# Probability blocks moved inside SBUF in 16 transfers on two queues, with two turn buffers and a lag of two

## The reference, cut to what matters

```python
s = jnp.einsum('bqgjd,bkgd->bgjqk', q5, kw)
p = masked_softmax(s, mw[None, None, None])
o_win = jnp.einsum('bgjqk,bkgd->bqgjd', p.astype(vw.dtype), vw)
...
o = g[..., 0:1] * o_cmp + g[..., 1:2] * o_sel + g[..., 2:3] * o_win
```

## Time and profile before

| | |
|---|---|
| median of 3 runs | 618.28 us |
| the profiled execution | 616.48 us, of which the span is 614.7 us |
| PE busy in the span | 565.3 us, 92% |
| DVE, ACT, POOL busy | 55%, 43%, 14% |
| p_turn written to DRAM | 16 units x 4 transfers, 64 KB to 256 KB each |
| read back | 16 transfers, 256 KB to 1 MB each |

### The profile page before, as it was taken

How to read it: one execution, slowest core, us unless ns; L and a number is a source line. 1 busy time by engine, 2 the same in 40 slices (tenths; PEclk the granted TensorE clock), 3 DMA queues, 4 the chain that set the end, 5 groups by cost and what they waited for, 6 DMA issues and landing times.

```text
span 614.7 us, 12596 instructions
## 1 busy us (share of the span) xinstructions
PE 565.3 (92%) x5102; PEld 506.0 (82%) x5102; DVE 335.5 (55%) x826; ACT 266.1 (43%) x601; POOL 88.6 (14%) x145
## 2 busy tenths in 40 slices
PE   6899999999889999988999998998895999998993
PEld 4899999999788998886897785766573999997992
DVE  5632213787776672364374575665663347762265
ACT  5543435446223433442332676466573342222333
POOL 0015432121101223603300000000001000000000
PEclk9999999999879999999999998999897999999998
DMA  8347822452334244842822177777685533307103
GB/s 296 153 120 231 263 69 95 165 187 87 104 100 178 81 129 144 278 159 89 290 69 70 40 202 239 220 219 225 200 227 127 143 90 86 111 12 238 38 2 145
DMA packets 70026, 90.98 MB, mean 148 GB/s; under 512 B 5457, under 2 KB 57873, under 8 KB 69714
## 3 DMA queue, kind: packets, MB, share of 16 engines
q1 hardware_dynamic: 59520, 55.34, 29.6%
q0 software_dynamic: 9728, 33.72, 16.5%
q10 hardware_dynamic: 722, 1.12, 0.5%
HBM read 75.71 MB, written 18.61 MB: 153 GB/s over the span
## 4 chain that ended last, share of the span: by engine, by line
PE 41%; DMA 11%; DVE 9%; ACT 3%; SPq 3%; issue 2%; ACTq 0%; DVEq 0%
PE m L1649 29%; DMA p_dram<-p_turn 9%; DVE p_turn L1560 3%; SPq L768 3%; PE t L1858 1%; PE s L1831 1%; PE s L1832 1%; PE s L1834 1%; DMA U<-in_x_p 1%; PE t L1795 1%; PE o L1917 1%; DVE w_lo L1231 1%; DMA p_slot<-p_dram 1%; PE s L1872 1%; PE o L1963 1%
## 5 line engine op out<-in xcount | busy, mean ns | idle before, releaser
L1649 PE MATMUL m<-h_hi,w_hi 128*128 128x272 f32 x448 | 135.1, 302 | 0.5 <-DVE w_lo L1231 0.5
L1649 PE MATMUL m<-h_hi,w_lo 128*128 128x272 f32 x448 | 130.1, 290 | 0.0
L1649 PE MATMUL m<-h_lo,w_hi 128*128 128x272 f32 x448 | 129.7, 290 | 0.0
L1649 PE MATMUL m<-w_hi,h_hi 128*128 128x256 f32 (+2 forms) x360 | 104.6, 291 | 4.4 <-DVE U L1597 2.0
L1649 PE MATMUL m<-w_lo,h_hi 128*128 128x256 f32 (+2 forms) x360 | 101.9, 283 | 0.0
L1649 PE MATMUL m<-w_hi,h_lo 128*128 128x256 f32 (+2 forms) x360 | 101.9, 283 | 0.0
L1231 DVE TENSOR_TENSOR w_lo<-raw,w_hi 128x1024 fp32r<-128x1024 f32 (+2 forms) x62 | 71.2, 1154 | 46.4 <-ACT w_hi L962 46.3
L1649 PEld LDWEIGHTS m<-h_hi,w_hi 128*128 128x128 f32 x448 | 85.4, 191 | 12.9 <-issue 10.4
L1649 PEld LDWEIGHTS m<-h_lo,w_hi 128*128 128x128 f32 x448 | 85.6, 191 | 0.0
L1649 PEld LDWEIGHTS m<-h_hi,w_lo 128*128 128x128 f32 x448 | 85.4, 191 | 0.0
L1649 PEld LDWEIGHTS m<-w_hi,h_hi 128*128 128x128 f32 (+1 forms) x360 | 67.9, 189 | 6.2 <-DVE U L1597 2.3
(11 more groups left out here) (304 smaller groups left out, 950.2 us busy)
## 6 DMA issues: line engine op xcount, KB each, us to landing
raw<-in_w_in SPq DMA_DIRECT2D x36, 512.0 KB, 4.5
U<-in_x_p SPq DMA_DIRECT2D x8, 512.0 KB, 7.3
p_dram<-p_turn SPq DMA_DIRECT2D x16, 256.0 KB, 5.1
raw<-in_w_o SPq DMA_DIRECT2D x8, 512.0 KB, 3.7
U<-p_dram POOLq DMA_DIRECT2D x3, 1024.0 KB, 6.3
p_dram<-p_turn SPq DMA_DIRECT2D x16, 192.0 KB, 4.8
U<-p_dram POOLq DMA_DIRECT2D x3, 768.0 KB, 5.1
raw<-in_w_in SPq DMA_DIRECT2D x8, 256.0 KB, 3.4
```

The source lines that it names most:

```text
L1649: ins = mm(out, lhs(a, k), rhs(b, k), start=(k == 0 and a + b == 0), stop=(k == n - 1 and a == 1))
```

## The change

The trip through DRAM goes. Square rows of the turn buffer (32 partitions: quarter a) go straight to quarter b of the slot. For each of the 16 pairs (a, b) there is one transfer of 32 partitions x (number of blocks) x 128 elements; SP issues ten of them (b = 0, 1 and half of 2), POOL six, each on semaphores of its own, and whoever waits for a unit waits for both. There are two turn buffers; the second takes the place of the fourth slot, so there are three slots. `pp` (u) is put two rounds after `ps` (u) instead of three.

```diff
-LAG = 3
+LAG = 2
+NSLOT, BY_SYNC = 3, 10
...
-LAST_TURN = (0, 1, 2)
+LAST_TURN = (1, 2)
...
+        def block_move(u, n):
+            b, a = divmod(n, 4)
+            kt = UNITS[u][0] + 1
+            src = p_turn[u % 2][32 * a:32 * a + 32, 0:512 * kt].rearrange("p (k b n) -> p k b n", k=kt, b=4)[:, :, b, :]
+            dst = slot[u % NSLOT][32 * b:32 * b + 32, 0:512 * kt].rearrange("p (k a n) -> p k a n", k=kt, a=4)[:, :, a, :]
+            return dst, src
+        def wait_moved(eng, u):
+            eng.wait_ge(p_moved[u % NSLOT], 16 * BY_SYNC * (u // NSLOT + 1))
+            eng.wait_ge(p_moved_pool[u % NSLOT], 16 * (16 - BY_SYNC) * (u // NSLOT + 1))
...
-                    sp.wait_ge(p_turned, u + 1)
-                    for a in range(4):
-                        sp.dma_start(p_dram[u, 0:nb, :, a * P:(a + 1) * P].rearrange("b j r -> j b r"),
-                                     p_turn[32 * a:32 * a + 32, 0:nb * P].rearrange("j (b r) -> j b r", b=nb)).then_inc(p_written, 16)
+                    sp.wait_ge(p_turned, s[1] + 1)
+                    for n in range(BY_SYNC):
+                        sp.dma_start(*block_move(s[1], n)).then_inc(p_moved[s[1] % NSLOT], 16)
...
-                    pool.wait_ge(p_written, 64 * (u + 1))
-                    pool.dma_start(slot[u % 4][:, 0:512 * (i + 1)].rearrange("p (k n) -> p k n", k=i + 1),
-                                   p_dram[u, 0:4 * (i + 1), :, :].rearrange("(k b) j n -> (b j) k n", b=4)).then_inc(p_moved[u % 4], 16)
+                    pool.wait_ge(p_turned, s[1] + 1)
+                    for n in range(BY_SYNC, 16):
+                        pool.dma_start(*block_move(s[1], n)).then_inc(p_moved_pool[s[1] % NSLOT], 16)
...
-                            dve.wait_ge(p_used, u - 3)
+                            dve.wait_ge(p_used, u - NSLOT + 1)
...
-                    dve.wait_ge(p_written, 64 * u)
+                    if u >= 2:
+                        wait_moved(dve, u - 2)
...
-                        pe.wait_ge(p_moved[u % 4], 16 * (u // 4 + 1))
+                        wait_moved(pe, u)
```

More of the change, by code:

```diff
@@ L553, in nsa_gmlp_layer @@
         SEL, WIN, CMP = 0, 1056, 1600
-        slot = [U[:, 0:2048], U[:, 2048:4096], U[:, 4096:6144],
-                nc.alloc_sbuf_tensor_at("p_slot", [P, 2048], F32, offset=wsT_at)[:, :]]
+        slot = [U[:, 0:2048], U[:, 2048:4096], U[:, 4096:6144]]
         pb = [x.rearrange("p (j k) -> p j k", j=J) for x in slot]
         p_blocks = [x.rearrange("p (k a j g r) -> p k a j g r", k=NT, a=4, j=2, g=G) for x in slot]
-        p_turn = nc.alloc_sbuf_tensor_at("p_turn", [P, 2048], F32, offset=prm_at)
+        p_turn = [nc.alloc_sbuf_tensor_at("p_turn0", [P, 2048], F32, offset=prm_at),
+                  nc.alloc_sbuf_tensor_at("p_turn1", [P, 2048], F32, offset=wsT_at)]
         ctb = [pm("b_sp"), tmp[:, :, :].rearrange("p a c -> p (a c)")[:, 0:512]]
-        p_dram = nc.dram_tensor("p_dram", [len(UNITS), 4 * NT, 32, 512], F32).ap()
         cp = U[:, 6144:6144 + J * G * NCP]
@@ L593, in nsa_gmlp_layer @@
         pads_zero, st_ready, mix_fn, pv_part = sem("pads_zero"), sem("st_ready"), sem("mix_fn"), sem("pv_part")
-        p_weight, p_turned, p_written, p_used, c_used = sem("p_weight"), sem("p_turned"), sem("p_written"), sem("p_used"), sem("c_used")
-        p_moved = [sem(f"p_moved{n}") for n in range(4)]
+        p_weight, p_turned, p_used, c_used = sem("p_weight"), sem("p_turned"), sem("p_used"), sem("c_used")
+        p_moved = [sem(f"p_moved{n}") for n in range(NSLOT)]
+        p_moved_pool = [sem(f"p_moved_pool{n}") for n in range(NSLOT)]
         ssq_ready, root_in, root_done, h_ready = sem("ssq_ready"), sem("root_in"), sem("root_done"), sem("h_ready")
@@ L1130, in _ @@
                     for j in range(J):
-                        ins = nc.scalar.activation(pb[u % 4][:, j, 0:n], pb[u % 4][:, j, 0:n], ACT.Exp, bias=st[:, m + 4 + j:m + 5 + j],
+                        ins = nc.scalar.activation(pb[u % NSLOT][:, j, 0:n], pb[u % NSLOT][:, j, 0:n], ACT.Exp, bias=st[:, m + 4 + j:m + 5 + j],
                                                    scale=SCALE, accum_out=st[:, m + 8 + j:m + 9 + j])
@@ L1556, in _ @@
                     dve.wait_ge(p_scaled, u + 1)
-                    dve.wait_ge(p_written, 64 * u)
+                    if u >= 2:
+                        wait_moved(dve, u - 2)
                     for j in range(J):
-                        dst = p_turn[:, 0:nb * P].rearrange("p (b j r) -> p b j r", b=nb, j=J)[:, :, j, :]
-                        ins = v.transpose(dst, pb[u % 4][:, j, 0:32 * nb].rearrange("p (b r) -> p b r", b=nb))
+                        dst = p_turn[u % 2][:, 0:nb * P].rearrange("p (b j r) -> p b j r", b=nb, j=J)[:, :, j, :]
+                        ins = v.transpose(dst, pb[u % NSLOT][:, j, 0:32 * nb].rearrange("p (b r) -> p b r", b=nb))
                     ins.then_inc(p_turned, 1)
```

12 lines of the change are left out of this document (4 added, 8 removed).

## The result

The changed kernel takes **636.32 us**, median of 4 runs (633.89 to 639.19), where the kernel before took 619.34 in the same comparison: a ratio of 1.0267 with a 95% interval from 1.0205 to 1.0330. It is slower, and its median lies above the forecast range of 611 to 633. Its profiled execution took 637.37 us, with a span of 635.6.

What follows compares the result with a forecast made beforehand. PE was the largest part, its DMA stage paced by the ring of turn, four issues, last landing, next turn. Stretches summed to -0.9 us, the clock added 4.4: 616.5 + 3.5 = 620.0 profiled, 621.8 us median, range 611 to 633.

Steps and rivals of the forecast that it cites:

- The move takes 0.03 + 9 spacings + landing: From a turn's end until `pp` may start, SP's ten transfers decide: 7.3, 7.0, 6.7 and 6.4 us for four to one block.
- Landing of 3.0 to 2.1 us: Time from an SP transfer's issue start to its landing: 3.0, 2.7, 2.4 and 2.1 us for four to one block.
- rival B: Moves are quick, spacing near 0.34 and landing 2 us or less: 607 to 612, say 611 us; chance 0.18.
- POOL's six end earlier: POOL's six transfers of a move take 5.5 us and end before SP's ten, even with another 0.5 us.
- The ring of two rounds: From `pp` (u) to `pp` (u + 2): 14.8 us with two blocks, 12.9 with one, slower than the ring it replaces.
- -3.7 us to the turn of unit 4: Four-block stretch: the turn of unit 4 starts at 389.6, where it was 393.35, a gain of 3.7 us.
- The three-block item: Stretch to unit 8: 31.2 us of PE work and waits of 1.8, 1.0, 2.1 give 35.8 for 35.71, +0.1 us.
- Behind 483.9 us PE runs on without a pause: After the stage's end PE never pauses, so what the stage gains or loses passes to the end.
- The clock, +4.4: In the stage, three of four PE waits of 2.1 to 2.3 us bring a slow clock costing 1.5 us each: +4.4 us.
- 1 us on every move is 7 us: Steepness: 1 us more on every move costs 1 us per two rounds, 7 us over 14 rounds.
- C: SP's issues are slow, 0.60 us and more, or pile up: +10 to +15 us, 631 us; chance 0.30.
- D: No difference, as PE's waits only change their place: 617 to 619 us; chance 0.10.

Runs made afterwards that it cites:

- kernel with short issues: Changed kernel with SP's ten transfers reading an input in DRAM in four-block units and writing to DRAM in the others (products' data wrong): 616.40 us, ratio 0.9983.
- the kernel with three layouts: Changed kernel with SP's ten transfers as writes to DRAM in three layouts by unit, every fourth unit staying SBUF to SBUF (products' data wrong): 628.97 us.

## Why the prediction was wrong, point by point

- **DVE's wait for the write goes**: right. 1.5 us are left, in the last unit.
- **The move takes 0.03 + 9 spacings + landing**: the form is right, its main term was mis-sized, and this is the step that failed. Spacing was taken as 0.47, from the nearest row in form, a write to DRAM; it is 0.635 (0.60 and 0.04 between). Ten transfers are 1.5 us longer for it. The bound of 0.65 from the earlier trace rows was right, and the working's own price for it, 12 us, would have given 632 us for a profiled execution and 634 for the median. "Nearest in form" counted partitions and runs; that one end was in DRAM counted more.
- **Landing of 3.0 to 2.1 us**: too long in the middle, by 0.3 to 0.5. Measured medians on SP are 2.6, 2.2, 1.9 and 1.8 us for four to one block. But what counts is the landing of the tenth, and it spreads: 2.0 to 3.7 us with four blocks and 1.9 to 2.6 with two. Unit 2 had 3.7, so its move took 9.6 us for 7.3, and PE waited 3.70 us for it. Why these were longer was not tried. Nor was the landing in SBUF shorter than that of a write to DRAM, which rival B counted on.
- **What the sum had not**: some bursts contain one issue of 0.8 to 1.4 us (1.25 in unit 13), of unknown cause; and where turns come faster than 6.35 us, the rest of the last unit's issues stands ahead (1.35 us for unit 14). With these, the moves that PE waited for took from 7.7 us (unit 6) to 9.6 us (unit 2), where 7.0 and 7.3 were forecast, and that of unit 14 took 8.9 for 6.4.
- **POOL's six end earlier**: right. They land 5.6 to 5.8 us after the turn in the four-block units, where 5.5 was forecast and SP's ten take 7.9 to 9.6, and no engine is recorded as waiting for them.
- **The ring of two rounds sets the pace in small units**: right in mechanism, 14.8 forecast and 17.7 measured. 1.9 us of the difference is the move. The rest is the clock (`pp` 1.97 for 1.01, the group 3.89 for 3.2), less what shorter masks and scores gave back.
- **-3.7 us to the turn of unit 4**: wrong by the same term, and by the landing of 3.7 us in unit 2. It came at 394.18, not at 389.6. With eight transfers on SP, or with short issues, this stretch took 37.35 and 37.14 us, so the step itself was right.
- **The three-block item** adds 31.2, 1.8, 1.0 and 2.1 us to 35.8; they make 36.1. The table above keeps the 35.8.
- **"Behind 483.9 us PE runs on without a pause"**: so for 56.7 us; in the last 74.1 us of the kernel before PE stands still for 13.3 us. What the stage lost passed to the end all the same, with 1.5 us more.
- **The clock, +4.4**: about right for the changed kernel, 3.4 measured as PE's extra busy time. But the length of the wait, which it was hung on, does not settle it, as PE's `pp` of units 5, 7 and 13 show:

```profile
413.50 1.52 PE L1973 MATMUL o<-U,v_tok 128*64 128x256 f32 x12 [2.16 <-DMA U<-p_turn]
430.99 2.83 PE L1973 MATMUL o<-U,v_tok 128*64 128x256 f32 x12 [2.70 <-DMA U<-p_turn]
487.57 0.65 PE L1973 MATMUL o<-U,v_tok 128*64 128x256 f32 x4 [4.30 <-DMA U<-p_turn]
```

  After 2.16 us a three-block `pp` took its usual 1.52 us, and after 2.70 us it took 2.83, at the lower level of the clock. After 4.30 us the one-block `pp` of unit 13 took its usual 0.65. So the figure of 3.4 is near the forecast's, but the rule behind it, a slow `pp` for each wait of 2 us, was not borne out: that the two figures are close is in part luck.
- **"1 us on every move is 7 us"**: too low. The moves of units 0 to 14 were 1.5 us longer on average than forecast, which at that rate is 11 us, but PE's waits came out 17.6 us above the forecast's -0.9. From the kernel with short issues to the changed one the moves grow by 2.0 us on average and the stage by 22.2 (152.1 for 129.9), again some 11 us for each; the lower clock and SP's full queue are in that figure and were not told apart.
- **The rivals**: C happened, slow issues with the ring longer and the clock falling, at 636 in place of its 631. Its condition (0.60 and more, deciding from 0.55) was met, and its price was too low. B and D are out.

By the Trainium skill (page "DMA: Bandwidth & Descriptors", section "Rules for kernel authors") small transfers should be joined. The changed kernel agrees in the outcome, 2.7% slower with sixteen transfers, but the price lay in issuing them: with eight on each queue (1.0047) or with short issues (0.9983) a kernel with the same number of transfers is within 0.5% of the kernel before. The same page's section "Issuing engines are not separate DMA queues" calls the time that a sequencer needs to initiate a transfer usually small relative to the transfer. Here it is not small: an issue is 0.60 us where its landing is 1.8 to 2.6, and over a burst nine spacings are 5.7 us of a move.

## What to carry to other kernels

When one transfer becomes many, the path gets (number - 1) x spacing + one landing, and the spacing must come from a row with the same two ends, not just the same shape; without one, the dearer bound is the safer choice. Then divide over the queues so that they end together: two transfers moved from SP to POOL were worth 14 to 16 us. And let the lag fit the unit: a shorter one is cheap where PE has much work in a round and dear where it has little.

## What the runs showed of the hardware

- An issue on SP takes 0.60 us when both ends are in SBUF (32 partitions, within a quarter or across, 16 to 64 KB; 0.62 with 64 partitions and 0.63 with 128), and 0.43 us from DRAM, or to DRAM in separate rows. A write to DRAM into one unbroken stretch of 64 KB takes 0.60 again. Why is open.
- On POOL the same transfers take 0.54 us to issue (0.55 for 64 KB, 0.50 for 16), less than on SP.
- A move within SBUF lands 2.6 us after its issue starts for 64 KB and 1.8 us for 16 KB, no sooner than a write to DRAM of the same shape (2.3 us for 64 KB, 1.8 for 48 KB in the kernel with three layouts, where 48 KB inside SBUF took 2.2 in the changed kernel).
